# Spatial gate tiles taken among the last S5 input products, and the first operator block loaded in two halves

## The reference, cut to what matters

```python
u, v, g_a, xs, g_b = jnp.split(h @ w_in, ...)             # width 512 each
# mixer A: chunked spatial gate
v = _layer_norm(v, v_g)
vc = v.reshape(Bn, L // CHUNK, CHUNK, A_GROUPS, A_GROUP_W)  # chunks of 128 tokens, 4 groups of 128
mixed = jnp.einsum('gpq,bnqgc->bnpgc', w_s, vc) + b_s.T[None, None, :, :, None]
y_a = u * mixed.reshape(Bn, L, A_WIDTH) * silu(g_a)
# mixer B: S5, 32 groups of 16 channels, 64 complex states, forward and backward
bu = einsum('blgh,gph->blgp', xs_groups, b_bar)           # real and imaginary
h = associative_scan(...)                                 # along the tokens
y = einsum(h, c) + d_skip * xs
```

## Time and profile before

| | us |
|---|---|
| median of 3 runs | 1246.27 (1244.56 to 1247.89) |
| time of the profiled execution | 1246.22 |
| its span, first to last instruction | 1244.4 |
| PE busy | 1192.2 (96%) |
| DVE busy | 809.6 (65%) |
| ACT busy | 510.8 (41%) |
| POOL busy | 447.2 (36%) |
| 16 DMA engines, mean traffic | 104 GB/s |
| mean granted TensorE clock | 0.992 of full speed |

### The profile page before, as it was taken

One profiled execution on the slowest core, in us unless ns is written; L12 is line 12 of the kernel. 1 busy time (PEld: TensorE's weight loads), 2 busy tenths in 40 slices (PEclk: granted clock), 3 DMA queues, 4 the chain that ended last, 5 costly groups with the idle time before them and its releaser, 6 DMA issues.

```text
span 1244.4 us, 17217 instructions
## 1 busy us (share of the span) xinstructions
PE 1192.2 (96%) x6722; PEld 981.4 (79%) x6722; DVE 809.6 (65%) x1266; ACT 510.8 (41%) x946; POOL 447.2 (36%) x346
## 2 busy tenths in 40 slices
PE   3899999999999999999999999989999999999997
PEld 2678789888889848878888888867888888887885
DVE  5699839899816263147659692258778777875227
ACT  3445456110016231144434331256666666665012
POOL 4700000000000003333113111268998899888232
PEclk9899999999999999999999999989999999999999
DMA  9935776435421951213022113220000000000303
GB/s 341 340 111 157 190 208 232 149 107 203 160 79 57 364 204 55 68 68 135 1 68 68 34 61 119 77 84 9 18 9 18 9 18 9 18 9 9 137 33 135
DMA packets 81024, 129.85 MB, mean 104 GB/s; under 512 B 12944, under 2 KB 43024, under 8 KB 80144
## 3 DMA queue, kind: packets, MB, share of 16 engines
q1 hardware_dynamic: 71120, 113.96, 27.2%
q10 hardware_dynamic: 9824, 14.80, 3.5%
HBM read 97.81 MB, written 30.93 MB: 103 GB/s over the span
## 4 chain that ended last, share of the span: by engine, by line
PE 80%; DVE 10%; DMA 4%; POOL 3%; issue 2%; ACT 2%; SPq 0%; POOLq 0%; DVEq 0%; ACTq 0%
PE ps L1812 9%; PE ps L1814 9%; PE ps L1813 9%; PE ps L1823 5%; PE ps L1825 5%; PE ps L1824 5%; DVE region_d L1081 3%; PE ps L2094 3%; DMA weight_ring<-in_w_mod 3%; PE ps L2130 3%; PE ps L2131 3%; PE ps L2132 3%; PE ps L2119 2%; PE ps L2116 2%; PE ps L2118 2%; PE ps L2117 2%
## 5 line engine op out<-in xcount | busy, mean ns | idle before, releaser
L662 POOL TENSOR_TENSOR region_b<-region_b,region_d 128x512 f32<-128x512 f32 x20 | 26.3, 1328 | 478.6 <-DVE region_d L1475 478.6
L1812 PE MATMUL ps<-w_hi,a_hi 128*128 128x512 f32 x448 | 177.7, 397 | 4.5 <-DVE b_lo L1169 3.8
L1813 PE MATMUL ps<-w_lo,a_hi 128*128 128x512 f32 x448 | 175.4, 391 | 0.0
L1814 PE MATMUL ps<-w_hi,c_lo 128*128 128x512 f32 x368 | 143.3, 389 | 0.0
L1571 DVE TENSOR_REDUCE small<-ps 128x1 f32<-128x1280 f32 x64 | 95.1, 1486 | 74.0 <-PE ps L2094 74.0
L1823 PE MATMUL ps<-a_hi,w_hi 128*128 128x512 f32 (+1 forms) x384 | 138.0, 359 | 0.0
L1824 PE MATMUL ps<-b_lo,w_hi 128*128 128x512 f32 (+1 forms) x384 | 136.1, 354 | 0.0
L1825 PE MATMUL ps<-a_hi,w_lo 128*128 128x512 f32 (+1 forms) x384 | 136.0, 354 | 0.0
L655 POOL TENSOR_TENSOR w_lo<-weight_ring,w_hi 128x2048 fp32r<-128x2048 f32 x14 | 65.1, 4651 | 185.6 <-ACT w_hi L711 185.6
L684 POOL TENSOR_TENSOR region_c<-region_c 128x512 f32<-128x512 f32 x80 | 110.1, 1377 | 30.5 <-ACT region_c L1053 28.2
L1812 PEld LDWEIGHTS ps<-w_hi,a_hi 128*128 128x128 f32 x448 | 84.8, 189 | 23.8 <-issue 5.8
(11 more groups left out here) (234 smaller groups left out, 2755.7 us busy)
## 6 DMA issues: line engine op xcount, KB each, us to landing
weight_ring<-in_w_mod SPq DMA_DIRECT2D x10, 2048.0 KB, 9.2
weight_ring<-in_we_in SPq DMA_DIRECT2D x10, 1024.0 KB, 5.7
weight_ring<-in_wo_in SPq DMA_DIRECT2D x10, 1024.0 KB, 5.1
weight_ring<-cop_t_scratch SPq DMA_DIRECT2D x4, 1536.0 KB, 7.9
region_c<-in_w_mod SPq DMA_DIRECT2D x2, 2048.0 KB, 20.2
bop_scratch<-region_d ACTq DMA_DIRECT2D x16, 256.0 KB, 2.9
cop_t_scratch<-region_d SPq DMA_DIRECT2D x8, 512.0 KB, 7.5
weight_ring<-bop_scratch SPq DMA_DIRECT2D x2, 2048.0 KB, 9.7
```

What stands on the lines that cost most here:

```text
L1812: te.matmul(o, th, wh[:, k % 4], start=k == 0, stop=False)
L1813: te.matmul(o, th, wl[:, k % 4], start=False, stop=False)
L1814: last = te.matmul(o, tl, wh[:, k % 4], start=False, stop=k == KT - 1)
```

## The change

It does four things. The gate's matmuls become a function `spatial_gate(tiles)`. TensorE calls it for the tiles 0 to 2 after xs product 9, for 3 and 4 after xs product 10, and for 5 to 9 after product 11. Its banks are now 2, 3 and 6 by turns (`GMB`), and a tile waits for DVE to be done with the tile three before; the wait for all twelve copies of xs is gone. The load `("bop", 0)` is made of two DMAs of 1024 KB, the first with a semaphore of its own (`s_bop_half`), for which B steps 0 to 7 wait; steps 8 to 15 wait for the second. Last, `u_in` has a semaphore for the first two blocks, one for the third and one for the fourth, waited for at steps 0, 16 and 24; and B step 2, whose bank 2 the gate now uses, waits for DVE to be done with all ten gate tiles.

```diff
+        GMB = (2, 3, 6)
...
                     src = bop_d[b].rearrange("p r g m -> p (r g m)")
+                    if b == 0:
+                        dst, src = dst.rearrange("p (r g m) -> p r g m", r=2, m=P), bop_d[b]
+                        sp.dma_start(dst[:, :, 0:8], src[:, :, 0:8]).then_inc(s_bop_half, 16)
+                        dst, src = dst[:, :, 8:16], src[:, :, 8:16]
...
-                              xs_d[fb].rearrange("s (c g) n -> (s c) g n", g=8)).then_inc(s_u_in if fb < 3 else s_u_in3, 16)
+                              xs_d[fb].rearrange("s (c g) n -> (s c) g n", g=8)).then_inc(s_u_in[max(fb - 1, 0)], 16)
...
-                    last = v.scalar_tensor_tensor(out=vt[:, t, fs], in0=ps[:, 4 + t % 2, fs], scalar=vgain[:, g:g + 1], in1=bsb[:, fs],
+                    last = v.scalar_tensor_tensor(out=vt[:, t, fs], in0=ps[:, GMB[t % 3], fs], scalar=vgain[:, g:g + 1], in1=bsb[:, fs],
...
+            def spatial_gate(tiles):
+
+                if tiles[0] == 0:
+                    pe.wait_ge(s_ws_ev, 1)
+                    pe.wait_ge(s_bl_ev, 16)
+                for t in tiles:
+                    pe.wait_ge(s_vg_ok, t + 1)
+                    if t >= 3:
+                        pe.wait_ge(s_gm_ok, t - 2)
+                    for g in range(FB):
+                        last = te.matmul(ps[:, GMB[t % 3], P * g:P * g + P], vt[:, t, P * g:P * g + P], wsT[:, g], start=True, stop=True)
+                    last.then_inc(s_gm_mm, 1)
...
                 between_tiles(after_xs.get(j, ()))
-
-            pe.wait_ge(s_ws_ev, 1)
-            pe.wait_ge(s_vg_ok, TT)
-            pe.wait_ge(s_xs_ev, 12)
-            for t in range(TT):
-                if t >= 2:
-                    pe.wait_ge(s_gm_ok, t - 1)
-                for g in range(FB):
-                    last = te.matmul(ps[:, 4 + t % 2, P * g:P * g + P], vt[:, t, P * g:P * g + P], wsT[:, g], start=True, stop=True)
-                last.then_inc(s_gm_mm, 1)
+                if j in (9, 10):
+                    spatial_gate(range(3) if j == 9 else range(3, 5))
+            spatial_gate(range(5, TT))
 
             pe.wait_ge(s_k_ev, 4)
             for j in range(32):
                 q, r = divmod(j, 2)
-                u = arrived("bop", q // 8)
+                if j < 8:
+                    pe.wait_ge(s_bop_half, 16)
+                    u = ("bop", 0)
+                else:
+                    u = arrived("bop", q // 8)
                 op = slot(u).rearrange("p (r g m) -> p r g m", r=2, m=P)
-                if j == 0:
-                    pe.wait_ge(s_u_in, 16 * 3)
-                if j == 24:
-                    pe.wait_ge(s_u_in3, 16)
+                if j % 8 == 0 and j != 8:
+                    pe.wait_ge(s_u_in[max(j // 8 - 1, 0)], 16 if j else 32)
+                if j == 2:
+                    pe.wait_ge(s_gm_ok, TT)
```

More of the change, by code:

```diff
@@ L291, in build @@
         s_xs_out = [sem(f"xs_out{i}") for i in range(2)]
-        s_u_in, s_u_in3, s_gb_in, s_y_in, s_y_in3, s_k_dd, s_ga_half, s_pchain, s_exp, s_v_nm = (
-            sem("u_in"), sem("u_in3"), sem("gb_in"), sem("y_in"), sem("y_in3"), sem("k_dd"), sem("ga_half"), sem("pchain"), sem("exp"), sem("v_nm"))
+        s_u_in, s_bop_half = [sem(f"u_in{i}") for i in range(1, FB)], sem("bop_half")
+        s_gb_in, s_y_in, s_y_in3, s_k_dd, s_ga_half, s_pchain, s_exp, s_v_nm = (
+            sem("gb_in"), sem("y_in"), sem("y_in3"), sem("k_dd"), sem("ga_half"), sem("pchain"), sem("exp"), sem("v_nm"))
         ld_x = [sem(f"ld_x{i}") for i in range(5)]
```

## The result

| | before | with the change |
|---|---|---|
| median, us | 1246.24 (20 runs, 1243.87 to 1249.88) | 1251.11 (20 runs, 1247.42 to 1253.45) |
| profiled execution, us | 1246.22 | 1247.86 |
| its span, us | 1244.4 | 1246.1 |

The ratio is 1.0031, 95% interval 1.0022 to 1.0041: slower, by about 0.3%. The forecast was 1250.4, with a range of 1246.4 to 1251.8. The time is near it, but the profile shows that two of the steps behind it were not as forecast.

The account below looks back on a forecast made before the run. TensorE, busy 96% of the span, with DVE pacing gate and B steps and a just-in-time load chain to step 16. Sum: 1246.22 + 1.9 (late second block) + 2.3 (clock) = 1250.4 us, range 1246.4 to 1251.8.

Parts of the forecast that it names:

- Product 11 ends 4.5 us later: Last xs product on TensorE: five gate tiles ahead of it, 0.9 us each, move its end to near 187.1.
- Second half: B steps from 16: store lands 2.4 us later, second block at 206.5, TensorE starts 2.45 later, copies shift 1.9 us.
- the bounds of 0 to 4.5: Fourth xs store's landing: shift 0 if engines finish the same bytes by 194.4, 4.5 us if it keeps its 11.2.
- First half of the B products: Steps 0 to 15: half block lands at 192 to 193.5, DVE's B copies start at 193.8, 2.6 us earlier.
- one of the three signs that I had named for being wrong: First half block landing after 194, moving the stall to step 0; others: store by 194.4, clock 1.00 behind the stall.
- The new waits on TensorE cost nothing themselves: Added semaphore waits on TensorE: 0 us, since every other thing they name is done by then.
- The clock term: TensorE idle 5.0 us before step 16, then lower clock for 4.8 us of work: loss 2.3 us, bounds 0 to 2.7.
- The cover of 0.5 us: Step 16: DVE absorbs 0.5 us of TensorE's 2.45 us later start, so the copies shift by 1.9 us.
- The Trainium skill's price for a DMA: Load chain to step 16: 2.0 us plus bytes over 436 GB/s, 8.3 us per pair; second block at 203.9.
- The rival that the DMA engines make up the delay: Second block lands at 204.05 as before, TensorE idles 2.5 us, time 1246.2; chance 0.10.
- the lower bound: Store's shift 0: engines, busy with small stores' leftovers and `u_in` before, work through the same bytes to the same end, 194.4.
- The faster rival: B products run on without a stall, second block landing by 201.5: 1246.2 - 2.6 = 1243.6; chance 0.04.

Follow-up runs that it names:

- e3: The change with the fourth U load issued by SP, ahead of the second operator block, instead of by ACT; ratio 1.0044.
- e6: The change with spare matmuls, results unused, on TensorE: 12 ahead of B step 0 and 12 ahead of step 4; ratio 1.0033.
- e8: e4 with both halves of the first operator block issued only when the fourth xs store has landed; ratio 1.0031.
- e11: e8 with the fourth U load issued by SP behind the second operator block instead of by ACT; ratio 1.0014.
- e1: The change with the first operator block loaded whole again, the gate still moved; ratio 1.0025.
- e13: The change, five gate tiles still ahead of product 11, with the DMAs in the order of e11; ratio 1.0024.
- e9: e8 with the first operator block loaded whole, behind the fourth xs store's landing; ratio 1.0037.
- e4: The change with all ten gate tiles behind product 11, in the three banks; the halves stay; ratio 1.0009.
- e12: e11 with the first half of the first block in two quarters, steps 0 to 3 waiting for the first alone; ratio 1.0004.
- e14: e4 with the first operator block loaded whole; ratio 1.0002.
- e5: e4 with only the second half of the first operator block issued after the fourth xs store has landed; ratio 1.0012.

## Why the prediction was right, and where it was not

The time and the direction were right, and so was the main cause: the fourth xs store and the second operator block start at product 11, and five gate tiles ahead of it delay them. Point by point:

- Product 11 ends 4.5 us later: 13.8 to 18.3 from product 9's start. Right. DVE takes the first five tiles in its idle time, and the last five in 5.26 us (said: 5.4). Right.
- "Second half": a shift of 2.4 us for the store, taken from the pair of second block and U load. It was 4.1. The gate's part alone was 2.9 to 3.2; the rest is the halves, which I had costed at nothing for the store, while the block takes 1.6 to 2.0 us longer in them. From rows 8 I read only that the store might gain. The shift sat inside the bounds of 0 to 4.5, and its value was mis-sized. The second block took 10.1 us for the 9.6.
- "First half of the B products": the first half block was to land 5 to 6 us after its issue and took 7.0, and step 0 came 0.8 us sooner than before and DVE's first copy 1.1, where I had DVE's copies 2.6 us sooner. On the clock of before that landing is at 194.1, and TensorE idled 2.63 us for it ahead of step 0: one of the three signs that I had named for being wrong came true. It had no effect on the end, since the second block was later still.
- "The new waits on TensorE cost nothing themselves": of what is queued behind a wait I looked at TensorE and SP and not at ACT, whose copies stand behind its wait for the store. That put 2.03 us of idle time at step 4 and left none at step 16, so the picture I gave of the profile was wrong there. e3 shows that it did not change the end.
- The clock term, 2.3 us: the clock did fall, as the rows on idle spells said, but behind the first stall and not behind one at step 16. It was back from about 203.2, and the steps it slowed had the second block still ahead of them. e6 shows its cost as 0.1 us, and it cannot have been more than 0.5. Its size was fair where nothing covers it: against the 9.2 us of before, 2.3 us more between step 0 and step 16 in e8, 2.5 in e11.
- The cover of 0.5 us was about right: step 16 came 5.0 us later and the first g_b product 4.6.
- So the sum, 1.9 + 2.3 = 4.2 against 4.6 measured in the stretch, came out near by luck, by two errors against each other: the shift of the load was too small by 2.6 us (2.45 for 5.0 at step 16), and the clock's 2.3 us were counted where they were covered. Only its first part is a mechanism that the runs bear out. The terms given for the forecast's own range also add up to 1249.1 to 1251.3, not to 1251.8; no conclusion hangs on it.
- The Trainium skill's price for a DMA (page "DMA: Bandwidth & Descriptors", section "Anatomy of one DMA — SWDGE (gpsimd) path"), 8.3 us for each pair, would have given no loss. The trace disagrees: 10.7 us for the store beside its load and 10.1 for the second block beside its own.
- The rival that the DMA engines make up the delay: a part, 1.5 us of the 4.5, was made up where the block stayed whole (e1 against before: 10.5 us from product 11 to the store's landing, 12.0 before). The reason may be the one given for the lower bound: before, the third U load landed 3.6 us after the block's issue, in e1 0.4 us ahead of it. e11 and e13, where no operator load stands beside the store, differ in the same way (5.2 and 3.5 us). That this load is the cause fits the rows, but no run changed it alone. The faster rival needed a landing that none of the kernels reached with the gate ahead.

What stays open: why the second block lands 9.4 to 10.4 us after the store from kernel to kernel where the first block was issued before the store. Its bytes are the same, and single executions do not tell spread from cause.

## What to carry to other kernels

Before moving work into an engine's busy stretch, list what starts at the end of that stretch: a store and the load that waits for it can be a longer chain than the work that is saved, and shares of the chain of waits don't name a transfer that is just in time. When one wait is removed, look on every engine, the one that issues DMAs beside its arithmetic too, for what is queued behind the wait that comes next. And a transfer that others wait for should not share the engines with a larger one: here the same store took 3.5 to 5.2 us without the operator block and 9.7 to 12.3 beside all of it. But then the larger one is late: in e8, e9 and e11 step 0 had to wait for it, and nothing was gained.

## What the runs showed of the hardware that I had not expected

- A smaller packet on one queue did not bring the other's transfer in sooner. Before, from 187 to 190 us, the whole block's 73 packets carried 1.20 MB beside 69 of the store's. In e4, with halves, from 185 to 188 us, SP's queue and ACT's also moved about equal numbers, now of 3.9 KB in place of 16.4:

```profile
q1 hardware_dynamic: 185, 0.73, 87.0%
q10 hardware_dynamic: 160, 0.10, 10.7%
```

  The store got the larger turn (0.10 MB against 0.04 in 3 us) and still landed 1.2 us later than before.
- Turns are not the whole of it. In the change the store was issued at 185.35, behind nothing on ACT's queue, and no packet of it shows until 190.6, while SP's queue moved 0.97 MB of the block; the second and third line are SP's queue and ACT's from 190.6 to 194:

```profile
q1 hardware_dynamic: 238, 0.97, 70.9%
q1 hardware_dynamic: 286, 1.09, 78.5%
q10 hardware_dynamic: 416, 0.27, 24.5%
```

  In e13, with no load beside it, the same store's issue and landing were 3.5 us apart. What holds its first packet back in the change is not shown.
- A load of 1 MB with nothing on the other queue took 7.0 us in e11, with three more loads issued behind it on its own queue; one of 512 KB took 5.0 in e12.
- How long an idle spell TensorE's clock bears is not one number here. It held after 2.27 us and after 2.32 (e4), and fell after 2.28 (e14 and e5), 2.56 (e3) and 2.63 (the change); and it fell up to 1.2 us after the work had begun again: in the change the work starts at 191.78 and the clock is 0.96 from 192 to 193 and 0.50 from then on.
